# Feed-forward, RWKV and convolution layers on one Trainium2 core: a down tile moved into the up block, nine products removed, five weight loads issued later

## The reference

```python
for i in range(2):                      # first block
    h = rms_norm(x, mixer_norm[i])
    x = x + (dsa_mixer(h, ...) if i == 0 else rwkv7_mixer(h, mu, w_rkv, w0, w1, w2, a0, a1, a2, g1, g2, ...))
    x = x + sqrelu_mlp(rms_norm(x, mlp_norm[i]), w_up[i], w_down[i])   # relu(h @ w_up)**2 @ w_down, d_ff = 4096
x = rms_norm(x, final_norm)
for i in range(2):                      # second block
    shift, scale, gate = split(silu(c) @ w_mod[i] + b_mod[i], 3)       # w_mod: 1024 x 3072
    h = rms_norm(x, norm_g[i]) * (1 + scale) + shift
    x = x + gate * (short_conv_mixer(h, w_in, ...) if i == 0 else dilated_mixer(h, w_in, ...))
return rms_norm(x, final_g)
```

## Time and profile before

| | before |
|---|---|
| median of 3 runs | 1079.24 us |
| profiled execution, span | 1078.37 us, 1076.7 us |
| TensorE busy | 1050.7 us (98%), 10195 products |
| VectorE busy | 767.8 us (71%) |
| ScalarE busy | 589.7 us (55%) |
| GpSimd busy | 120.5 us (11%) |
| loads from memory | 189.45 MB, 177 GB/s over the span |
| a granule of down weights, issue to landing | 5.9 us (median) |
| a third of a modulation column, issue to landing | 7.5 us (median) |
| low-rank weights | 256, 256, 640, 256 and 256 KB, issued from 118.7 to 122.2 us |

### The profile page before, as it was taken

One profiled execution on the slowest core, in us unless ns is written; L12 is line 12 of the kernel. 1 busy time (PEld: TensorE's weight loads), 2 busy tenths in 40 slices (PEclk: granted clock), 3 DMA queues, 4 the chain that ended last, 5 costly groups with the idle time before them and its releaser, 6 DMA issues.

```text
span 1076.7 us, 24929 instructions
## 1 busy us (share of the span) xinstructions
PE 1050.7 (98%) x10195; PEld 985.5 (92%) x10199; DVE 767.8 (71%) x1088; ACT 589.7 (55%) x900; POOL 120.5 (11%) x131
## 2 busy tenths in 40 slices
PE   9989999999999999998999999999999999999987
PEld 8966999999999789997899999999997999998875
DVE  6987657655789688767756666795676887875675
ACT  6685555555456783243555554553534667665552
POOL 0220200100000028841000010000000000000000
PEclk9999999999999999999999999999999999999999
DMA  8724777786635410001676777747554656566401
GB/s 319 243 81 138 236 261 269 272 284 244 234 123 155 159 60 4 4 23 61 215 271 220 260 267 276 277 119 224 181 171 135 208 172 214 172 215 185 146 2 39
DMA packets 83069, 192.16 MB, mean 178 GB/s; under 512 B 6000, under 2 KB 6912, under 8 KB 82992
## 3 DMA queue, kind: packets, MB, share of 16 engines
q1 hardware_dynamic: 74256, 159.93, 45.2%
q0 software_dynamic: 7584, 27.53, 7.6%
q10 hardware_dynamic: 1152, 3.59, 1.0%
HBM read 189.45 MB, written 1.05 MB: 177 GB/s over the span
## 4 chain that ended last, share of the span: by engine, by line
PE 84%; DVE 7%; DMA 3%; ACT 3%; issue 2%; POOL 0%; DVEq 0%; POOLq 0%; SPq 0%; ACTq 0%
PE bank L2254 14%; PE bank L2258 14%; PE bank L2259 14%; PE bank L2555 5%; PE bank L2556 5%; PE bank L2554 5%; PE bank L2230 5%; PE bank L2232 5%; PE bank L2231 5%; PE bank L2766 3%; DVE w_lo L1340 1%; PE bank L2878 1%; DMA mod_w<-in_w_mod_dram 1%; DMA raw<-in_dsa_w_in_dram 1%; DVE mx_d L2164 1%
## 5 line engine op out<-in xcount | busy, mean ns | idle before, releaser
L732 ACT ACTIVATE w_hi<-raw 128x1024 fp32r<-128x1024 f32 x295 | 309.6, 1058 | 303.6 <-PE bank L2259 163.4
L1340 DVE TENSOR_TENSOR w_lo<-raw,w_hi 128x1024 fp32r<-128x1024 f32 x295 | 356.1, 1223 | 157.9 <-ACT w_hi L732 157.0
L2254 PE MATMUL bank<-act_hi,w_hi 128*128 128x256 f32 x1384 | 385.7, 279 | 1.1 <-issue 0.7
L2258 PE MATMUL bank<-act_lo,w_hi 128*128 128x256 f32 x1384 | 384.5, 278 | 0.0
L2259 PE MATMUL bank<-act_hi,w_lo 128*128 128x256 f32 x1384 | 384.2, 278 | 0.0
L2254 PEld LDWEIGHTS bank<-act_hi,w_hi 128*128 128x128 f32 x1384 | 259.8, 188 | 4.2 <-issue 2.8
L2258 PEld LDWEIGHTS bank<-act_lo,w_hi 128*128 128x128 f32 x1384 | 259.7, 188 | 0.1
L2259 PEld LDWEIGHTS bank<-act_hi,w_lo 128*128 128x128 f32 x1384 | 259.6, 188 | 0.0
L2554 PE MATMUL bank<-w_hi,ff_hi 128*128 128x256 f32 x512 | 142.5, 278 | 0.0
L2555 PE MATMUL bank<-w_lo,ff_hi 128*128 128x256 f32 x512 | 142.5, 278 | 0.0
L2556 PE MATMUL bank<-w_hi,ff_lo 128*128 128x256 f32 x512 | 142.5, 278 | 0.0
(11 more groups left out here) (359 smaller groups left out, 1336.0 us busy)
## 6 DMA issues: line engine op xcount, KB each, us to landing
raw<-in_mlp_w_up_dram SPq DMA_DIRECT2D x64, 512.0 KB, 4.5
raw<-in_mlp_w_down_dram SPq DMA_DIRECT2D x64, 512.0 KB, 5.9
raw<-in_dil_w_in_dram SPq DMA_DIRECT2D x64, 512.0 KB, 4.1
mod_w<-in_w_mod_dram POOLq DMA_DIRECT2D x48, 512.0 KB, 7.5
raw<-in_conv_w_in_dram SPq DMA_DIRECT2D x32, 512.0 KB, 4.4
raw<-in_rwkv_w_rkv_dram SPq DMA_DIRECT2D x24, 512.0 KB, 3.9
raw<-in_dsa_w_in_dram SPq DMA_DIRECT2D x12, 512.0 KB, 5.9
raw<-in_dsa_w_o_dram SPq DMA_DIRECT2D x8, 512.0 KB, 4.6
```

The costliest lines, as they stand in the source:

```text
L732: act.activation(w_hi[:, slot, :], raw[:, slot, :], ACT.Copy).then_inc(hi_ready, 1)
L1340: dve.tensor_tensor(w_lo[:, slot, :], raw[:, slot, :], w_hi[:, slot, :].bitcast(F32), ALU.subtract).then_inc(lo_ready, 1)
L2254: pe.matmul(dst, w_hi[:, slot, at], hi[:, kt, :], start=begin, stop=False, skip_group_check=True)
L2258: pe.matmul(dst, w_hi[:, slot, at], lo[:, kt, :], start=False, stop=False, skip_group_check=True)
```

## The change

There are three edits.

1. In steps 1 to 6 of both feed-forward blocks the first tile of the down block (granule 0, token tile 0, first half of the output: six products) is issued inside the fourth granule of the up block, ahead of its last feature group (`held`, `f == 3`). The tile's waits, for the down granule's `lo_ready` and for `mid_lo`, come with it. `down` skips that tile there.
2. The nine spare products are removed, three in each of `rwkv_in`, `conv` and `dilated`.
3. `load_lora` is called from `modulation(0)`, behind the loads of column 2. POOL's loop over columns 1 to 7 becomes two loops, 1 to 2 and 3 to 7. The wait for `x_updated` stays ahead of the first load.

```diff
-            def modulation(l):
+            def modulation(l, between=None):
...
-                with pool.Fori(1, KT) as k:
-                    for n in range(3):
-                        pool.wait_ge(mod_used[n], k + done)
-                        load(n, k)
+                def columns(first, last):
+                    with pool.Fori(first, last) as k:
+                        for n in range(3):
+                            pool.wait_ge(mod_used[n], k + done)
+                            load(n, k)
+
+                columns(1, 3)
+                if between is not None:
+                    between()
+                columns(3, KT)
 
             def load_lora():
-                pool.wait_ge(x_updated, 4)
...
-            load_lora()
-            modulation(0)
+            pool.wait_ge(x_updated, 4)
+            modulation(0, load_lora)
...
                 for f in groups:
+                    if held is not None and f == 3:
+                        held()
...
-                        if across is not None and f == kk == 0:
-                            for x, w in ((hi, w_hi), (hi, w_lo), (lo, w_hi)):
-                                pe.matmul(across[:, 0:SEQ], x[:, kt, 0:P], w[:, slot, 0:SEQ], start=True, stop=True)
...
                             for n in range(2):
-                                mm = down_tile(i, n, q, (base + k0 + q) % RING, slot, first, False)
+                                if first or q + i + n:
+                                    mm = down_tile(i, n, q, (base + k0 + q) % RING, slot, first, False)
                         mm.then_inc(granule_used, 1)
+
+                def first_tile(it, k0, slot):
+
+                    wait_down(it, k0, 0)
+                    down_tile(0, 0, 0, (base + k0) % RING, slot, False, False)
...
-                    feature_block(base, 4, hi, lo, (bank[0], bank[1]), it)
+                    feature_block(base, 4, hi, lo, (bank[0], bank[1]), it, None if first else lambda: first_tile(it, 8, 0))
                     down(it, 8, 0, first)
...
-                            feature_granule(g, g % RING, hi, lo, q, banks, across=bank[6] if n == 0 and q == 2 else None)
+                            feature_granule(g, g % RING, hi, lo, q, banks)
```

More of the change, by code:

```diff
@@ L2240, in token_granule, with feature_granule @@
                 mm.then_inc(granule_used, 1)
-            def feature_granule(g, slot, hi, lo, q, banks, groups=range(4), inc=True, across=None):
+            def feature_granule(g, slot, hi, lo, q, banks, groups=range(4), inc=True, held=None):
                 if inc:
@@ L2267, in token_block, with feature_block @@
                                   banks, q == 0, q == PER_BLOCK - 1)
-            def feature_block(base, k0, hi, lo, banks, it=None):
+            def feature_block(base, k0, hi, lo, banks, it=None, held=None):
                 for q in range(PER_BLOCK):
-                    feature_granule(number(base, k0 + q, it), (base + k0 + q) % RING, hi, lo, q, banks)
+                    feature_granule(number(base, k0 + q, it), (base + k0 + q) % RING, hi, lo, q, banks,
+                                    held=held if q == PER_BLOCK - 1 else None)
             def turn(n, src, ordered=False):
@@ L2974, in conv @@
                             g = base + 16 * half + 4 * n + q
-                            feature_granule(g, g % RING, hi, lo, q, (bank[2 * n], bank[2 * n + 1]), across=bank[6] if n == half == 0 and q == 2 else None)
+                            feature_granule(g, g % RING, hi, lo, q, (bank[2 * n], bank[2 * n + 1]))
                 pe.wait_ge(conv_x, 2)
@@ L2992, in pair @@
                             wait_act(6, q)
-                            feature_granule(number(base, 4 * n + q, it), (base + 4 * n + q) % RING, hi, lo, q, (bank[2 * n], bank[2 * n + 1]),
-                                            across=bank[6] if isinstance(it, int) and n == 0 and q == 2 else None)
+                            feature_granule(number(base, 4 * n + q, it), (base + 4 * n + q) % RING, hi, lo, q, (bank[2 * n], bank[2 * n + 1]))
                 pair(0)
```

## The result

The changed kernel took 1089.95 us (median of 4 runs, 1089.4 to 1090.63) against 1079.95 us (4 runs) of the kernel before: ratio 1.0087, 95% interval 1.0058 to 1.0116. In a later group of 12 runs it had 1087.68 us against 1082.89, ratio 1.0034 (1.0007 to 1.0061). (The ratios are estimated from the single runs; they differ a little from the quotient of the medians.) It is slower, by 0.3 to 0.9%. The forecast was 1079.0 and its range ended at 1084.5: both were wrong. One execution of the changed kernel with a profile took 1090.0 us, span 1088.3.

A forecast was written before the change was run, and what follows sets the result against it. TensorE, busy 98% of the span, was taken as the bound, with products at 113.3 or 117.8 ns. Terms -1.0 - 3.2 + 4.9 - 2.2 + 1.3 = -0.2 us gave 1079.0 us, chance 0.30; 8-in-10 range 1071.5 to 1084.5.

The forecast's parts named there:

- Nine spare products, -1.0: In the three mixers: removing the nine products saves 0.36 us per three, -1.0 us in all.
- Conv_in stays fast, -3.2: Conv_in starts at 113.3 ns a product and, without its spare products, keeps that for 719 products: -3.2 us.
- Dilated_in, +4.9: Dilated_in starts slow after a wait and, without spare products, 1,102 products stay at 117.8 ns: +4.9 us.
- The double passage, -2.2: Block 1: two up-to-down passages per step leave only 72 slow products instead of 576: -2.2 us.
- I take no wait, barely: Block 1: the fourth up granule's chain fits its 18.02 us, with a margin of 0.04 to 0.85 us.
- thin margins fail: Rival, chance 0.28: block 1's fourth up granule is late in step 2 or 3, then slow products; +1.6, total 1082.8 us.
- Block 0, +1.3: Block 0: wait at 160 us gone, new wait near 203 us, 168 more slow products; net +1.3 us.
- TensorE would wait at about 203 us, between 0 and 2 us; I take 0.9: Block 0: late low-rank loads push back step 2's last down granule and column 3's loads; TensorE waits 0.9 us.
- The term for the slow products, 168 more: Block 0: after the wait near 203 us, slow to the block's end, 768 slow products against 600; 168 x 4.45 ns.
- without that wait: -2.7: Block 0 without the wait near 203 us: only 72 slow products, -2.7 us.
- The wait at 160 us, -0.4: Block 0, step 1: low-rank loads out of the way bring column 1 earlier, so TensorE's wait goes: -0.4 us.
- After a wait on up products the rate is slow: Feed-forward blocks: after TensorE waits on up products, they take 117.8 ns each, not 113.3.

The follow-up runs named there:

- five kernels with tile and move: Down tile inside the up block, plus VectorE's third modulation product moved behind `ff_lo`, with or without the other parts; ratios to the kernel before 0.9906 to 0.9957.
- the kernel before with only the move: Kernel before with only VectorE's third modulation product moved from ahead of the fourth up granule's rest to behind `ff_lo`; 1082.7 us, ratio 1.0022.

## Why the prediction was wrong, step by step

Over the stages the profile was 11.9 us above the forecast: 4.4 in block 0, 2.7 in block 1, 3.5 in conv_in, 0.85 in the RWKV mixer and 0.4 ahead of block 0. The last two are within what these stages vary (the RWKV mixer took 230.7 to 231.8 us in the 14 profiles). Two steps failed: the waits of block 0, and the margin of block 1, which took conv_in with it.

- **Nine spare products, -1.0.** Right in size where it could be read (0.36 us a triple).
- **Conv_in stays fast, -3.2. Failed**, in the clause "nothing before it in the diff touches its entry". The gain itself is real: 87.13 us in every profile without the triple whose block 1 ended fast. But the entry takes the rate with which block 1 ends, in 14 of 14 profiles: slow in the three whose block 1 ended slow (the changed kernel twice, the tile alone), fast in the other eleven. The sum had the two as separate terms; they are one. A wait in block 1 costs the block's gain and conv_in's.
- **Dilated_in, +4.9.** Right in this pair, +4.5 with its triple gone, but by luck: what I read as a rule (slow after the wait) is a draw. The start was slow in 10 of 14 profiles and fast in 4, with no relation to conv_in's rate.
- **The double passage, -2.2.** Right as a mechanism: 176.27 us in all five kernels with tile and move, against 178.45. Over all profiles the rate turned at 302 of 302 passages from up to down products at the full clock (not at the two at half the clock) and at none of 272 back, those with a wait or at half the clock left out. **"I take no wait, barely" failed**: the margin of 0.04 to 0.85 us failed in the changed kernel at 642.30 and, in its second profile, at 599.49. The rival "thin margins fail" was the right case, and its mechanism with it: 0.2 to 0.3 us of wait, then slow to the block's end. With conv_in it had 1085.6.
- **Block 0, +1.3. The step that failed most in a single stage: "TensorE would wait at about 203 us, between 0 and 2 us; I take 0.9".** Place and cause were right, the size wasn't: 2.9 us and, by the fall of the clock, 1.5 more, and 0.7 in the waits at 182.11 and 231.64 with the product behind each. I had counted how much traffic is pushed back (1 to 2 us) and set it against the chain's overflow. The chain kept within its 18.02 us (17.34). What counts is when the one load lands for which it stands still: 5.0 us later. Before, this load had been served in the idle time that the low-rank loads now filled. The term for the slow products, 168 more, came out (172 more, 944 against 772 in the whole block), but by luck: they came in other places than I had them, from 182.11 to the half clock and from 231.64 on, with fast phases between. The end "without that wait: -2.7" was exact (176.53 against 179.20).
- **The wait at 160 us, -0.4.** It did go, but it wasn't there in the second profile of the kernel before either.
- **After a wait on up products the rate is slow.** Held in both blocks, behind 12 of 12 waits of 0.06 to 3.0 us between up products; in ten of them the rate had been fast. A granule 17 ns late didn't do it.
- **The range.** The margins that I had worked out were 0.04 and 0.11 us, read from one execution, and I treated each place as one independent unknown. The spread of 15 us between executions of one kernel shows that the places are drawn anew each time, and that one failure brings the next.

What stays open: why there are two rates at all; what draws the rate at dilated_in's start and in attention's 192 products; why a triple of activations-stationary products turned the rate in conv_in and dilated_in 12 times in 13 and in rwkv_in 2 times in 6. In the second profile of the changed kernel the rate also turned from slow to fast at about 195 us, behind a down product that came 31 ns late, with no passage near. No experiment here reaches any of these.

## To carry to other kernels

Where a product's rate depends on what ran before it, a wait is priced by the products behind it up to the next thing that turns the rate, here through a stage border too, and not by its own length: 0.09 us of wait cost 3.3 us in a block. A faster block has less room, so look first for what stands ahead of the released work on the helper engine (here one modulation product with a load behind it) and move that; the same change went from 0.3 to 0.9% slower to 0.65 to 0.94% faster by moving one product. Background loads placed in "idle" DMA time cost here what the next urgent load lost (5.0 us), not their share of the bandwidth.

## What the runs showed of the hardware

Behind the 2.74 and 2.87 us of idle time the granted clock fell to 0.50 only when TensorE had been running again for 0.7 to 1.2 us. Around the 2.02 us of idle time near 68 us, before the attention's transposed probabilities, it fell in nine of the 14 profiles and not in the other five, with the same code there, and in one of the nine (the kernel before with only the move) it fell 0.4 us before TensorE ran again. Here the changed kernel, and then the kernel before:

```profile
67.50:71.00 3.50, 2.22 (x14) 0.72 0.00 0
```

```profile
67.00:70.00 3.00, 0.98 (x11) 1.00 0.00 0
```

Medians of this kernel carry a draw of about 5 us from one stage: a difference between two versions is read from the stages of their profiles first, and from 12 runs rather than 3.
